# Two transformer blocks on one core: the second output projection by halves of the tokens, and the experts' tokens chosen by sorting chunks of 256

## What is computed

```python
x = x + gt1 * (concat([att, conv]) @ w_out)                  # second output projection
h2 = rmsnorm(x, g_ffn) * (1 + sc2) + sh2
aff = softmax(h2 @ w_router)                                 # 1024 x 16
g, idx = top_k(swapaxes(aff, 1, 2), 128)                     # each expert picks 128 tokens
xs = h2[idx]
y = (silu(xs @ w_gate[e]) * (xs @ w_up[e])) @ w_down[e] * g
x = x + gt2 * segment_sum(y, idx)
return rmsnorm(x, g_final)
```

## Time and profile before

| | us |
|---|---|
| median of 3 runs | 2703.43 (2700.7 to 2704.67) |
| the profiled execution | 2702.21 |
| its span | 2700.4 |

### The profile page before, as it was taken

The page is one execution under the profiler, slowest core; times in us unless marked ns, Lnnn a source line. Parts: engine busy times, 40 slices in busy tenths (PEclk is TensorE's granted clock), DMA queues, the critical chain, the costliest instruction groups (busy, mean ns, idle before and its releaser), DMA issues.

```text
span 2700.4 us, 34356 instructions
## 1 busy us (share of the span) xinstructions
PE 2508.4 (93%) x11874; PEld 1985.7 (74%) x11874; DVE 1626.8 (60%) x2499; ACT 1166.4 (43%) x1711; POOL 675.3 (25%) x401
## 2 busy tenths in 40 slices
PE   5999899978899989989989899999987899999996
PEld 2886467767678877777778678788864588888885
DVE  4122696656453346574542534488427899999997
ACT  4021353343443322343333421244223588888886
POOL 0211110013344467334456322410110011111100
PEclk9999899989899999899999899999988799999998
DMA  6010000022222254222222211100023999999995
GB/s 271 28 35 16 32 1 1 0 78 78 67 90 93 95 188 174 72 78 94 93 104 99 78 63 47 47 1 0 16 79 126 398 381 396 396 396 396 396 394 211
DMA packets 85913, 378.86 MB, mean 140 GB/s; under 512 B 7916, under 2 KB 9116, under 8 KB 71456
## 3 DMA queue, kind: packets, MB, share of 16 engines
q1 hardware_dynamic: 81072, 360.26, 35.2%
q0 software_dynamic: 4752, 17.43, 2.4%
HBM read 356.60 MB, written 21.05 MB: 140 GB/s over the span
## 4 chain that ended last, share of the span: by engine, by line
PE 65%; issue 16%; DVE 7%; POOL 7%; ACT 3%; DMA 1%; POOLq 0%; ACTq 0%; SPq 0%; DVEq 0%
PE ps L854 7%; PE ps L856 7%; PE ps L855 7%; PE ps L1110 6%; PE ps L1112 6%; PE ps L1111 6%; POOL w_lo L2168 5%; PE ps L687 5%; PE ps L679 3%; PE ps L824 2%; POOL a_lo L2172 2%; PE ps L744 2%; PE ps L746 2%; PE ps L745 2%; PE ps L1020 1%
## 5 line engine op out<-in xcount | busy, mean ns | idle before, releaser
L2168 POOL TENSOR_TENSOR w_lo<-arena,w_hi 128x1024 fp32r<-128x1024 f32 x180 | 438.3, 2436 | 804.8 <-ACT w_hi L1313 804.7
L2055 DVE TENSOR_TENSOR e_lo<-arena,e_hi 128x1024 fp32r<-128x1024 f32 x384 | 453.2, 1221 | 35.8 <-ACT e_hi L1536 23.2
L1536 ACT ACTIVATE e_hi<-arena 128x1024 fp32r<-128x1024 f32 x384 | 403.9, 1061 | 102.5 <-PE ps L1112 102.5
L854 PE MATMUL ps<-h_hi,w_hi 128*128 128x512 f32 x848 | 340.9, 402 | 32.3 <-POOL w_lo L2168 19.9
L1313 ACT ACTIVATE w_hi<-arena 128x1024 fp32r<-128x1024 f32 x180 | 189.8, 1055 | 398.9 <-PE ps L856 398.9
L856 PE MATMUL ps<-h_hi,w_lo 128*128 128x512 f32 x848 | 334.7, 395 | 0.0
L855 PE MATMUL ps<-h_lo,w_hi 128*128 128x512 f32 x848 | 334.6, 395 | 0.0
L854 PEld LDWEIGHTS ps<-h_hi,w_hi 128*128 128x128 f32 x848 | 162.0, 191 | 76.2 <-issue 30.6
L1110 PE MATMUL ps<-e_hi,x_hi 128*128 128x512 f32 x512 | 202.9, 396 | 4.0 <-DVE e_lo L2055 4.0
L1853 DVE SCALAR_TENSOR_TENSOR arena<-ps,cols,arena 128x511 f32<-128x511 f32 x88 | 63.8, 746 | 232.8 <-ACT arena L1378 232.8
L1112 PE MATMUL ps<-e_lo,x_hi 128*128 128x512 f32 x512 | 200.0, 391 | 0.0
(11 more groups left out here) (314 smaller groups left out, 4821.7 us busy)
## 6 DMA issues: line engine op xcount, KB each, us to landing
arena<-in_w_up SPq DMA_DIRECT2D x108, 1024.0 KB, 8.3
arena<-in_w_down SPq DMA_DIRECT2D x86, 1024.0 KB, 8.2
arena<-in_w_gate SPq DMA_DIRECT2D x64, 1024.0 KB, 9.8
arena<-in_w_in SPq DMA_DIRECT2D x18, 1024.0 KB, 4.8
arena<-in_w_ada SPq DMA_DIRECT2D x12, 1024.0 KB, 12.8
arena<-in_w_out SPq DMA_DIRECT2D x12, 1024.0 KB, 4.8
arena<-in_w_ada SPq DMA_DIRECT2D x24, 512.0 KB, 6.7
routed_rows<-arena SPq DMA_DIRECT2D x8, 520.0 KB, 2.6
```

The costliest lines, as they stand in the source:

```text
L854: pe.matmul(out, w_hi[:, q, w], hi, start=start, stop=False)
L1536: act_e.activation(e_hi[:, (2 * sl + a) % RING, :], slot[sl][:, a * D:(a + 1) * D], ACT.Copy).then_inc(s_ehi, 1)
L2055: v.tensor_tensor(e_lo[:, r, :], slot[sl][:, a * D:(a + 1) * D], e_hi[:, r, :].bitcast(F32), ALU.subtract).then_inc(s_elo, 1)
L2168: gp.tensor_tensor(w_lo[:, q, :], slot[c][:, q * D:(q + 1) * D], w_hi[:, q, :].bitcast(F32), ALU.subtract).then_inc(s_wlo, 1)
```

## The change

It has three parts.

- The second output projection goes by halves of the tokens, as the first does. Each of its 16 parts has its own weight split, so the weights are loaded and split twice. VectorE gates all parts. The norm of the first half, its scaling and shift, its logits and softmax, and the turning of the first eight row tiles (four of `xT`, four of `hT`, all through banks 4 and 5 and the two buffers `tok`) lie inside the second half's matmuls; `row_turn(j)` waits for `row_out(j-1)`. The other half of this work and the other eight row tiles follow the projection.
- The tokens are chosen in another way. The affinities are transposed so that each expert has four chunks of 256 tokens on four groups of 32 partitions. The 128 largest of each chunk are found in order (`ranked`), two chunks are merged by taking the maximum of one list and the other reversed, the result is sorted by seven stages of maximum and minimum, and a second merge gives the 128 largest, whose minimum is the threshold. Tokens above it are taken, and as many of those equal to it as there is room for. The second gate's addition stands after the second count.
- In the first output projection and at the start of the second block the additions of `branch_added` alternate with the sums of the next norm. ScalarE evacuates all parts of the projection's second half; one weight copy stands behind the last square; means and spreads have other places among the matmuls; the context's scaling and shift stand earlier.

Some tiles have other places in memory (`hT`, `tok`, `wr`, `lgT`, `silu_b`), and norm 12 becomes norms 12 and 13. The diff, cut:

```diff
                 sp.wait_ge(s_wlo, 2 * (G_OUT2 + g) - 2)
-                sp.dma_start(slot[(G_OUT2 + g) % 2], out2[:, g, :]).then_inc(s_wl[(G_OUT2 + g) % 2], 16)
+                sp.dma_start(slot[(G_OUT2 + g) % 2], out2[:, g % (KT // 2), :]).then_inc(s_wl[(G_OUT2 + g) % 2], 16)
+                if g == 1:
+                    sp.wait_ge(tps, 2 * T_OUT2)
+                    sp.dma_start(wr, T["w_router_2"][0].rearrange("(k p) e -> p k e", p=P)).then_inc(s_late, 16)
+                if g == KT - 2:
+                    store_row(0)
+            for j in range(1, 8):
+                store_row(j)
             wga = T["w_ada_2"].rearrange("l (k a p) n -> l k p a n", a=2, p=P)[0]
             sp.wait_ge(tps, 2 * (T_OUT2 + 8))
...
                 sp.dma_start(slot[i].rearrange("p (a n) -> p a n", a=2), wga[i][:, :, 5 * D:6 * D]).then_inc(wl[i], 16)
-            sp.wait_ge(evv, T_OUT2 + 8)
+            for j in range(8, 2 * NT):
+                store_row(j)
...
@@ -870,11 +881,10 @@
...
             output_part(KT, {5: lambda: mean(3)})
-            output_part(KT + 1, {2: lambda: spread(3)})
-            for i in range(2, 4):
+            output_part(KT + 1, {1: lambda: spread(3)})
+            for i in range(2, 5):
                 output_part(KT + i)
-            output_part(KT + 4, {7: lambda: mean(4)})
-            output_part(KT + 5, {4: lambda: spread(4)})
+            output_part(KT + 5, {2: lambda: mean(4), 7: lambda: spread(4)})
...
                 output_part(KT + i)
@@ -971,21 +981,21 @@
             pe.wait_ge(s_hhi, 3 * KT)
             pe.wait_ge(evv, T_IA - 3)
-            input_half(0, 0)
+            pe.wait_ge(eva, T_IA - 2)
+            input_half(0, 0, {1: lambda: mean(9)})
+            pe.wait_ge(evv, T_IA)
             pe.wait_ge(eva, T_IA)
-            mean(9)
-            pe.wait_ge(evv, T_IA)
-            input_half(0, 1, {4: lambda: mean(10)})
-            input_half(0, 2, {0: lambda: spread(9), 2: lambda: spread(10)})
+            input_half(0, 1, {2: lambda: spread(9), 6: lambda: mean(10)})
+            input_half(0, 2, {3: lambda: spread(10)})
             input_half(0, 3)
             input_half(0, 4)
-            input_half(0, 5, {1: lambda: mean(11), 6: lambda: spread(11)})
+            input_half(0, 5, {7: lambda: mean(11)})
...
+            spread(11)
...
@@ -1044,44 +1054,79 @@
             pe.wait_ge(evv, T_OUT2)
...
+            def output_part2(i, between={}):
+                t, h, half = T_OUT2 + i // 2, i % 2, i // KT
+                hs = slice(half * HALF, (half + 1) * HALF)
+                pe.wait_ge(s_wlo, 2 * G_OUT2 + i + 1)
+                tile_free(t, h)
...
+                    if k in between:
+                        between[k]()
+                    hi, lo = (o_hi, o_lo) if k < 4 else (c_hi, c_lo)
+                    m = passes(ps[:, 2 * (t % 2) + h, :], h, k, hi[:, k % 4, hs], lo[:, k % 4, hs], k == 0, k == KT - 1)
+                m.then_inc(tps, 1)
+            def row_turn(j):
+                h, t = row_tile(j)
+                src, bank = (hT if h else xT), (4 if j < 8 else 2 * (j % 2))
+                if j < 8 or j >= 10:
+                    pe.wait_ge(s_rte, j if j <= 8 else j - 1)
...
+                    m = pe.transpose(ps[:, bank + k // 4, (k % 4) * P:(k % 4 + 1) * P], src[:, k, t * P:(t + 1) * P], ident)
+                m.then_inc(s_rtp, 1)
+            def logits(half):
...
+                    pe.wait_ge(s_hb, (3 + half) * KT + k + 1)
+                    m = pe.matmul(ps[0:NE, 7, :], wr[:, k, :], hT[:, k, half * HALF:(half + 1) * HALF], start=(k == 0), stop=(k == KT - 1))
+                m.then_inc(s_lgT, 1)
...
+            for i in range(KT):
+                output_part2(i)
+            output_part2(KT, {4: lambda: mean(12)})
+            output_part2(KT + 1, {2: lambda: spread(12)})
+            for i in range(2):
+                output_part2(KT + 2 + i, {1: lambda: row_turn(2 * i), 5: lambda: row_turn(2 * i + 1)})
+            output_part2(KT + 4, {0: lambda: logits(0), 6: lambda: logit_rows(0)})
+            output_part2(KT + 5, {5: lambda: row_turn(4)})
+            output_part2(KT + 6, {1: lambda: row_turn(5), 5: lambda: row_turn(6)})
+            output_part2(KT + 7, {1: lambda: row_turn(7)})
+            mean(13)
+            pe.wait_ge(evv, T_OUT2 + 8)
+            pe.wait_ge(eva, T_OUT2 + 8)
+            row_turn(8)
+            row_turn(9)
+            spread(13)
+            logits(1)
+            row_turn(10)
+            logit_rows(1)
+            row_turn(11)
+            pe.wait_ge(s_aff, 2)
+            for r in range(2):
+                m = pe.transpose(ps[:, 7, r * P:(r + 1) * P], aff32[:, r * P:(r + 1) * P], ident)
+            m.then_inc(s_at, 1)
+            pe.wait_ge(s_rte, 8)
+                m = pe.transpose(ps[0:NE, 4 + i // 4, (i % 4) * P:(i % 4 + 1) * P], aff[:, i, :], ident)
+            for j in range(12, 2 * NT):
+                row_turn(j)
+            pe.wait_ge(s_rte, 2 * NT)
...
-                if i % 2:
-                    odd_part(i)
-                output_high(i + 2)
+                if i >= KT or i % 2:
+                    even_or_odd_part(i)
+                if i != KT - 1:
+                    output_high(i + 2)
             squares(3, lambda k: zT[0][:, k, :], lambda k: [(eva if k % 2 else evv, T_OUT + k // 2 + 1)], {k: (lambda k=k: next_part(k)) for k in range(KT)})
+            output_high(KT + 1)
             root(3)
             next_part(KT)
...
@@ -1354,13 +1401,13 @@
             root(4)
             next_part(KT + 4)
             spread(4)
-            part_at = {1: lambda: next_part(KT + 5), 5: lambda: output_high(KT + 8)}
+            part_at = {1: lambda: next_part(KT + 5), 5: lambda: next_part(KT + 6)}
...
-            odd_part(KT + 7)
+            even_or_odd_part(KT + 7)
...
@@ -1449,19 +1496,16 @@
...
-            squares(10, lambda k: yT[:, k, :], lambda k: [(evv, d), (eva, d)])
-            input_high(2)
-            root(9)
+            squares(10, lambda k: yT[:, k, :], lambda k: [(evv, d), (eva, d)], {3: lambda: root(9), 6: lambda: input_high(2)})
+            spread(9)
             root(10)
             part1(T_IA, vT[:, lo])
...
-            spread(9)
             spread(10)
             squares(11, lambda k: xT[:, k, hi], lambda k: [(s_x, 25 + k)],
-                    {2: lambda: input_high(4), 6: lambda: (part1(T_IA + 1, q2[:, 1, lo], HD ** -0.5), input_high(5))})
-            shift(35, hcT, 0, 1, range(4))
+                    {1: lambda: shift(35, hcT, 0, 1, range(4)), 2: lambda: input_high(4), 3: lambda: shift(35, hcT, 0, 1, range(4, KT)),
+                     4: lambda: (part1(T_IA + 1, q2[:, 1, lo], HD ** -0.5), input_high(5))})
             root(11)
-            shift(35, hcT, 0, 1, range(4, KT))
...
             spread(11)
...
+            def output2_high(i):
+                weight_high(G_OUT2 + i // 2, (i // 2) % 2, i % 2, (tps, 2 * T_OUT2 + i - 1))
+            def gated(i):
+                return [(eva if i % 2 else evv, T_OUT2 + i // 2 + 1)]
+            def shift_half(half, ks):
+                shift(51 + KT * half, hT[:, :, half * HALF:(half + 1) * HALF], 24, 0, ks)
...
+            def row_out(j):
+                h, t = row_tile(j)
+                act_e.wait_ge(s_rtp, j + 1)
+                if j >= 2:
+                    act_e.wait_ge(s_tkst[j % 2], 16 * (j // 2))
+                if h:
+                    act_e.wait_ge(s_aff, j // 8 + 1)
+                    act_e.activation(tok[j % 2][:, D:ROW], aff[:, t, :], ACT.Copy)
+                act_e.activation(tok[j % 2][:, 0:D], banks(4 if j < 8 else 2 * (j % 2), D), ACT.Copy).then_inc(s_rte, 1)
+            squares(12, lambda k: xT[:, k, lo], gated, {k: (lambda k=k: output2_high(k + 1)) for k in range(1, KT)})
+            output2_high(KT + 1)
+            root(12)
+            output2_high(KT + 2)
+            spread(12)
+            shift_half(0, range(4))
+            output2_high(KT + 3)
+            shift_half(0, range(4, KT))
+            squares(13, lambda k: xT[:, k, hi], lambda k: gated(KT + k),
+                    {1: lambda: (row_out(0), row_out(1), output2_high(KT + 4)), 2: lambda: (row_out(2), row_out(3), output2_high(KT + 5)),
+                     3: lambda: (logits_copied(0), router_exp(0), output2_high(KT + 6)), 4: lambda: (row_out(4), output2_high(KT + 7)),
+                     5: lambda: (row_out(5), row_out(6)), 6: lambda: row_out(7)})
+            root(13)
+            row_out(8)
+            row_out(9)
+            spread(13)
+            shift_half(1, range(KT))
+            logits_copied(1)
+            row_out(10)
+            router_exp(1)
+            for j in range(11, 2 * NT):
+                row_out(j)
...
@@ -1790,19 +1862,13 @@
             even_part(0)
             sums(3, {k: (lambda k=k: even_part(k)) for k in range(2, KT, 2)})
             diagonal(3)
-            even_part(KT)
             v.wait_ge(xld, 16)
             rs = spread_ready(3)
```

(75 more changed lines are left out.)

193 lines of the change are left out of this document (69 added, 124 removed).

## The result

The changed kernel takes 2688.35 us (median of 5 runs, 2688.08 to 2690.53), the kernel before 2704.67 (2700.7 to 2706.12): ratio 0.9942, 95% interval 0.9931 to 0.9952. The profiled execution took 2690.53 us with a span of 2688.7, against 2702.21 and 2700.4: 11.7 us less.

The account below looks back on a forecast made before the run. It took the 115.9 us between second output projection and experts, where TensorE never sets the pace for long, as the bound. -12 - 5 - 2 = -19 from 2702.2 gave 2683.2 profiled, 2684 median; range 2674 to 2696.

Parts of the forecast that it names:

- Projection: Second output projection: 16 us of added TensorE work and 5 of stop and slow clock, +21; bounds +16 to +35.
- no other stop: Second output projection: the replay found TensorE stopping only at the second row turn, for 3.3 us.
- the slow clock behind the stop: Second output projection: TensorE runs slowly for a while after the gap at the second row turn, 1.5 us.
- From the projection to the sort: Projection's end to the sort: only half the tokens are left, so 26 us, -12 against before.
- The sort: Choice of tokens: rounds on 256 columns, merges and tie counting take 27.0 us against 45.9, -18.9; bounds 24 and 34.
- Gate and counts: Before the experts: the gate ends before the positions and no longer holds VectorE; positions to first expert matmul 30.3 us.
- the early places: First output projection and start of the second block, forecast at -5 and -2 us.
- (3): Rival: row stores wait behind weight loads, the gate becomes the bound, gain 8 us less, 2692; chance 0.10.
- (4): Rival: seven of eight row turns stop TensorE inside the second output projection, slower at 2713; chance 0.04.
- First output projection: Moved weight copy, copies on ScalarE and alternating adds start the up projection 5 us earlier; bounds -8 to -1.
- the second inverse root comes 5 us earlier: First output projection: replayed step by which the up projection also starts 5 us earlier.
- Start of the second block: Low-part wait shrinks, 3.3 us of context scaling leave, part 0 starts later (2.3): -2 us, bounds -5 to +3.

Follow-up runs that it names:

- e6_turn_later: Changed kernel with row turns 1 to 3 of the second output projection 0.5 to 1 part later, ScalarE's row copies in that order: 2685.6 us.
- e7_tail: Changed kernel with silu products ahead of the second half's softmax, router_exp(1) ahead of row_out(10), and row turn 9 behind the spread of norm 13: 2685.6 us.
- e4_sort_alone: Kernel before with only the new choice of tokens and the gate's addition behind two counts; projections and second block start as before: 2704.4 us, ratio 0.9996.
- e10_stats_earlier: Changed kernel with norm 4's mean and spread earlier in TensorE's order of the first output projection (mean in part 12, spread heading part 13): 2686.5 us.
- e2_block2_undone: Changed kernel with the start of the second block as in the kernel before (statistics order, context scaling, sum 11 in one piece): 2686.9 us, ratio 0.9935.
- e5_copy_behind: Changed kernel with ScalarE's weight copy for part 2 of the second block's input projection moved back behind norm 10's eight squares: 2690.3 us.
- e8_alternate: Changed kernel with the old second block start, keeping only sum 11's alternation with residual additions and two context scalings ahead of the residual: 2687.0 us.

## Why the prediction came out as it did

The median lies in the range, 4 us above the forecast of 2684. The profiled execution, for which the terms were added up, took 2690.5 in place of 2683.2, so 11.7 us were gained of 19, and only 8.3 of them in the stages of the sum. The single terms are another matter.

**Projection.** +21 predicted, +23.4 measured. The place and length of the stop were right (row turn 1, 3.53 us against 3.3), and the replay's "no other stop" too. The added work came to 16.6 against 16: a row turn lengthens the distance between two projection matmuls (0.23 us) by 0.88, the logits by 7.2, mean and spread by 1.85 together, the small transposes by 0.5 (0.3 us of the 23.4 are not placed). Mis-sized was the slow clock behind the stop, 3.0 us and not 1.5; e6_turn_later gave back 6.1 of stop and clock. The rule of the Trainium skill that I weighed there ("GPSIMD Engine Reference", section Specifications) agrees with the rows of after as well: the eight scalings ahead of `shift_half(0)`, beside POOL's low parts, took 3.22 and 4.88 us in two groups of four, while the eight of the second half, with POOL idle, took 5.39 in all.

**From the projection to the sort.** 26 predicted, 25.0 measured, and each term within 0.7 us; e7_tail shows that the silu products, the table load and a row turn together did lie on the path (they were not tried one by one).

**The sort.** 27.0 predicted, 26.9 measured: the round 0.98 against 0.96, merges and threshold 4.3 against 4.6, the tail 7.0 against 7.1. By the formula of the Trainium skill that the prediction names ("VectorE: DVE Perf Modes", section "The TRN2 errata") a stage is estimated at 0.45, and the two operations of a round at 0.85; the 0.93 of the prediction holds 0.08 that the formula doesn't have. Measured were 0.38 (2.68 / 7), and 0.84 for the two operations (0.43 + 0.41) of a round of 0.98. Its advice on tiles of 512 elements did not decide here.

**Gate and counts.** Right: the gate was never late, and from the positions to the first expert matmul it took 30.6 us, forecast 30.3. That this matmul came at 2109.30, forecast 2109.3, is luck, and not even a hit: the forecast counted from a projection that starts where it did before (1917.8). With the -5 and -2 of the early places it should have come at 2102. Counted from the projection's first matmul it was 193.3 us against 191.5, and an entry 1.8 us earlier made up for it. Rivals (3) and (4) had no part in it; that the gate binds where the projection is not halved, e4_sort_alone showed.

**First output projection.** -5 predicted, -1.9 measured. The step that failed is the last of it: "the second inverse root comes 5 us earlier". It came 1.7 us earlier (89.8 us after the first matmul, 91.5 before), although the sum came 4.2 us earlier (76.6 against 80.8). I had moved the mean and the spread with it, though they stand in TensorE's order inside part 13; the change even moves the mean later, from part 12 to 13. With the mean put back, e10_stats_earlier gained 5.6.

**Start of the second block.** -2 predicted (bounds -5 to +3), +3.5 measured: the sign was wrong, and beyond the bound. I named the later start of part 0 and priced its stop (2.3, measured 2.38), but put the slow clock behind it at nothing, and it cost some 3 us; with it the mean and spread of norm 10, which stand in TensorE's order inside the next parts, come 6.8 and 5.7 us later than in e2_block2_undone. I had credited 3.3 us for the context scaling leaving the stretch behind the last sum, but there it lay in gaps and cost nothing; ahead of the residual it meets POOL (5.39 us) and holds the residual for 1.5. I missed what the weight copy at the seventh square is queued behind (it waits 3.39 us for part 0), worth 1.0 us by e5_copy_behind. And I let the alternating sum count in full, while TensorE meets its statistics at a fixed place (e8_alternate). That the stop of part 0 and its clock are the largest of these is read from the rows; no run undid that wait alone.

So the three places are not -12, -5, -2 but -9.9, -1.9 and +3.5. That the median still came within 4 us of the forecast is in part luck: of the 11.7 us between the profiled executions 3.4 lie in code that both kernels share, and the medians lie 16.3 apart, which the stages don't account for.

## What to carry to other kernels

An addition that comes earlier is worth nothing until the instruction that uses it stands earlier in its own engine's order: after moving a sum, move the mean, the diagonal and the spread, and look for the wait under its new name. Where two parts of a change stand in a row on two paths (here gate and sort), test each alone: one can be worth nothing, the other a loss, and both together the gain. A new stop of TensorE costs more than its length: 2.38 us at part 0 and 3.53 at row turn 1 each brought some 3 us of slow clock with them here, though the last section has stops that cost none. Starting credits and other signals without work behind them belong ahead of the long work beside them, not behind it (some 7 of the 9.3 us here, by the rows).

## What the hardware showed

**The same gap costs clock in one execution and in another it doesn't.** In after and in e7_tail the code up to here is the same; TensorE stands 1.96 and 1.95 us before part 12. Busy time by stretch, the granted clock being the third number from the end; first after, then e7_tail:

```profile
664.00:671.00 7.00, 5.32 (x24) 1.00 0.01 2
672.00:680.00 8.00, 8.00 (x27) 0.57 0.40 131
```

```profile
663.00:670.00 7.00, 6.82 (x23) 0.76 0.01 2
670.50:676.00 5.50, 5.50 (x29) 1.00 0.57 191
```

After the first gap it stayed at 1.00 in after and fell in e7_tail; in after it fell behind the next one (2.05 us), just where mean and spread of norm 4 lie on the path. Stage a differs by 3.3 us between two executions of one order, more than the change brought there. The same stands behind smaller differences in the table: stage d of e5_copy_behind is 1.5 us longer than in after, with the same stop of 2.49 us ahead of it, and the mean, two row turns and the spread behind it take longer (6.9 us from start to end, 5.4 in after).

**VectorE beside POOL.** A product of 0.75 us took 2.72 in after (1525.82), beside a low part that POOL made from 1525.61 to 1527.99, and even the diagonal, 0.69 otherwise, took 1.77 in e10_stats_earlier, beside the low part of a weight copied just before. Which instruction falls there is part of the price of every reordering; at the start of the second block it took back part of what the alternation saved.
